# A rotary query projection at half its width: the half-exchanged columns made by ScalarE copies of the projected tile

## The reference

```
q = (_rms(c_q, q_norm) @ w_uq).reshape(bsz, L, MLA_HEADS, MLA_NOPE + MLA_ROPE)
q_nope, q_rope = q[..., :MLA_NOPE], q[..., MLA_NOPE:]
...
half = x.shape[-1] // 2
x1, x2 = x[..., :half], x[..., half:]
return jnp.concatenate([x1 * cos - x2 * sin, x1 * sin + x2 * cos], axis=-1)
```

## Time and profile before

| | |
|---|---|
| median of 3 runs | 3479.05 us |
| span of the profiled execution | 3477.8 us |
| TensorE matmul busy | 3399.0 us (98%), 16886 instructions |
| VectorE busy | 1670.0 us (48%) |
| ScalarE busy | 1424.7 us (41%) |
| GpSimd busy | 667.1 us (19%) |
| mean granted TensorE clock | 0.994 |

### The profile page before, as it was taken

One profiled execution on the slowest core, in us unless ns is written; L12 is line 12 of the kernel. 1 busy time (PEld: TensorE's weight loads), 2 busy tenths in 40 slices (PEclk: granted clock), 3 DMA queues, 4 the chain that ended last, 5 costly groups with the idle time before them and its releaser, 6 DMA issues. The chain is left out here.

```text
span 3477.8 us, 44891 instructions
## 1 busy us (share of the span) xinstructions
PE 3399.0 (98%) x16886; PEld 2804.8 (81%) x16886; DVE 1670.0 (48%) x3074; ACT 1424.7 (41%) x2495; POOL 667.1 (19%) x487
## 2 busy tenths in 40 slices
PE   7999999999899999999999999999999999999999
PEld 6788888877688888788787878788788888887887
DVE  4899999637555655521403232232323415555311
ACT  5233322243276666510325545445554234555200
POOL 4221212111201111033221111110102113331231
PEclk9999999999999999999999999999999999999999
DMA  4333323377421211543323232323322543333532
GB/s 129 91 88 91 100 83 97 100 210 233 134 53 38 57 43 39 155 135 104 129 68 104 88 111 78 117 66 90 105 82 88 186 154 118 109 109 116 182 97 66
DMA packets 431590, 368.88 MB, mean 106 GB/s; under 512 B 73560, under 2 KB 366936, under 8 KB 431376
## 3 DMA queue, kind: packets, MB, share of 16 engines
q1 hardware_dynamic: 345936, 271.62, 27.0%
q10 hardware_dynamic: 85440, 94.39, 7.8%
HBM read 238.18 MB, written 127.75 MB: 105 GB/s over the span
## 5 line engine op out<-in xcount | busy, mean ns | idle before, releaser
L874 PE MATMUL ef_ring<-ef_hhi,ef_whi 128*128 128x512 f32 x744 | 298.0, 400 | 2.0 <-issue 1.0
L2715 ACT ACTIVATE eow_w1raw<-of_ring 128x512 f32<-128x512 f32 x218 | 126.6, 595 | 415.2 <-PE of_ring L3088 414.2
L876 PE MATMUL ef_ring<-ef_hhi,ef_wlo 128*128 128x512 f32 x744 | 290.6, 391 | 0.0
L875 PE MATMUL ef_ring<-ef_hlo,ef_whi 128*128 128x512 f32 x744 | 290.4, 390 | 0.0
L400 POOL TENSOR_TENSOR ef_wlo<-ef_wraw,ef_whi 128x1024 fp32r<-128x1024 f32 x30 | 89.0, 2966 | 499.6 <-ACT ef_whi L449 499.6
L874 PEld LDWEIGHTS ef_ring<-ef_hhi,ef_whi 128*128 128x128 f32 x744 | 139.9, 188 | 42.6 <-issue 14.9
L2934 DVE SCALAR_TENSOR_TENSOR of_state<-of_state,of_small,of_tv 128x256 f32<-128x256 f32 x64 | 56.1, 877 | 245.6 <-ACT of_tv L2777 243.5
L511 ACT ACTIVATE ef_stage<-ef_ring 128x512 f32<-128x512 f32 x93 | 55.3, 594 | 273.2 <-PE ef_ring L876 273.0
L876 PEld LDWEIGHTS ef_ring<-ef_hhi,ef_wlo 128*128 128x128 f32 x744 | 139.9, 188 | 30.1
L875 PEld LDWEIGHTS ef_ring<-ef_hlo,ef_whi 128*128 128x128 f32 x744 | 140.3, 189 | 27.2
L3762 PE MATMUL mh_pf<-mh_v,mh_pp 128*128 128x258 f32 x736 | 162.0, 380 | 0.0
(11 more groups left out here) (612 smaller groups left out, 9460.2 us busy)
## 6 DMA issues: line engine op xcount, KB each, us to landing
of_wraw<-o_w_in SPq DMA_DIRECT2D x53, 512.0 KB, 3.9
ef_wraw<-e_w_in SPq DMA_DIRECT2D x29, 512.0 KB, 4.2
s_tmo<-eow_w1raw ACTq DMA_DIRECT2D x48, 256.0 KB, 2.3
ow_raw<-s_yt SPq DMA_DIRECT2D x18, 512.0 KB, 6.2
ow_raw<-o_w_out SPq DMA_DIRECT2D x16, 512.0 KB, 5.1
s_uc<-ef_stage ACTq DMA_DIRECT2D x24, 256.0 KB, 2.6
ef_ut<-s_uc SPq DMA_DIRECT2D x16, 384.0 KB, 4.1
s_za<-ef_stage ACTq DMA_DIRECT2D x24, 256.0 KB, 2.3
```

The lines of the kernel that those rows point to most:

```text
L874: pe.matmul(out, ah, hhi[:, f, tc], start=(f == 0), stop=False)
L875: pe.matmul(out, ah, hlo[:, f, tc], start=False, stop=False)
L876: mm = pe.matmul(out, al, hhi[:, f, tc], start=False, stop=(f == KT - 1))
L2715: act.activation(stage[i % 4][:, :], ring[i % 3][:, :] if i else start.first, func, scale=GK ** -0.5 if name == "q" else 1.0).then_inc(eva ...
```

## The change

The second group of each rotary item is gone. TensorE projects an item once, nine matmuls in place of eighteen. The weight columns are loaded in another order, so that the 128 partitions of the projected tile are first half of head 2p, first half of head 2p+1, second half of head 2p, second half of head 2p+1, 32 partitions each. The exchange is then a swap of the two blocks of 64 partitions. ScalarE does it with two copies of 64 partitions each, from the PSUM tile to r2, scaled by a column of signs (`rope_swap`), since the signs of the sine table stand in the old order. VectorE multiplies the PSUM tile by the cosines into r1 as before, then r2 in place by the sines, and adds. The sign column is set by three small VectorE instructions at the start of the stage, in a tile that is not yet in use. A load of the weights of a pair is four transfers of 32 columns in place of two of 128, and a load of a head's rotary query is four transfers of 32 partitions in place of two of 64.

```
--- before.py
+++ after.py
...
@@ -1345,8 +1343,8 @@
         y_out = [s.sem(f"y_out{u}") for u in range(3)]
 
         wn = d["w_uq_nope"].rearrange("(k p) n -> p k n", p=P)
-        wr = d["w_uq_rope"].rearrange("(k p) n -> p k n", p=P)
-        wsw = d["w_uq_swap"].rearrange("(k p) n -> p k n", p=P)
+        wr = d["w_uq_rope"].rearrange("(k p) (q a x i) -> q x a p k i", p=P, a=2, x=2, i=32)
+        sign = st[0][:, 0:1]
         wkv = d["e_w_ukv"].rearrange("(k p) n -> p k n", p=P)
 
         def cut(c):
...
@@ -1398,8 +1396,10 @@
                     if p >= 2:
                         sp.wait_ge(rhi_done, p - 1)
                         sp.wait_ge(rlo_done, p - 1)
-                    for x, src in enumerate((wr, wsw)):
-                        sp.dma_start(rraw[p % 2][:, x, :, :], src[:, :, p * P:(p + 1) * P]).then_inc(rw_in[p % 2], 16)
+                    for x in range(2):
+                        for a in range(2):
+                            at = 64 * x + 32 * a
+                            sp.dma_start(rraw[p % 2][:, :, at:at + 32], wr[p, x, a]).then_inc(rw_in[p % 2], 16)
 
                 def rope_store(p, c):
                     i = roped["r", p, c]
...
@@ -1410,8 +1410,10 @@
                     if h:
                         sp.wait_ge(qr_hi, 2 * h)
                         sp.wait_ge(qr_done, 2 * h)
-                    for a in range(2):
-                        sp.dma_start(qrr[64 * a:64 * a + 64, :], d["qr"][h * ROPE:(h + 1) * ROPE, :]).then_inc(qr_in, 16)
+                    for x in range(2):
+                        at = h // 2 * P + 64 * x + 32 * (h % 2)
+                        for a in range(2):
+                            sp.dma_start(qrr[64 * a + 32 * x:64 * a + 32 * x + 32, :], d["qr"][at:at + 32, :]).then_inc(qr_in, 16)
 
                 def place(m):
                     h, t, _ = tile_of(2 * m)
...
@@ -1486,8 +1488,8 @@
                     u = p % 2
                     pool.wait_ge(rhi_done, p + 1)
                     if p >= 2:
-                        pool.wait_ge(rope_mm, 6 * (p - 1))
-                    pool.tensor_tensor(rlo[u][:, :, :, :], rraw[u][:, :, :, :], rhi[u][:, :, :, :].bitcast(F32), ALU.subtract).then_inc(rlo_done, 1)
+                        pool.wait_ge(rope_mm, 3 * (p - 1))
+                    pool.tensor_tensor(rlo[u][:, :, :], rraw[u][:, :, :], rhi[u][:, :, :].bitcast(F32), ALU.subtract).then_inc(rlo_done, 1)
 
                 def key_split(i):
                     t = cut(chunk[i])
...
@@ -1551,10 +1553,20 @@
                     act.activation(whv[:, :, :, :], vraw[:, :, :, :], ACT.Copy).then_inc(vhi_done, 1)
 
                 def rope_high(p):
-                    act.wait_ge(rw_in[p % 2], 32 * (p // 2 + 1))
+                    act.wait_ge(rw_in[p % 2], 64 * (p // 2 + 1))
                     if p >= 2:
-                        act.wait_ge(rope_mm, 6 * (p - 1))
-                    act.activation(rhi[p % 2][:, :, :, :], rraw[p % 2][:, :, :, :], ACT.Copy).then_inc(rhi_done, 1)
+                        act.wait_ge(rope_mm, 3 * (p - 1))
+                    act.activation(rhi[p % 2][:, :, :], rraw[p % 2][:, :, :], ACT.Copy).then_inc(rhi_done, 1)
+
+                def rope_swap(x):
+
+                    i = roped[x]
+                    act.wait_ge(rope_mm, i + 1)
+                    if i >= 2:
+                        act.wait_ge(rope_done, i - 1)
+                    for a in range(2):
+                        of, to = slice(64 * (1 - a), 64 * (2 - a)), slice(64 * a, 64 * (a + 1))
+                        act.activation(r2[i % 2][to, :], ring[slot[x] % 3][of, :], ACT.Copy, scale=sign[of, :]).then_inc(swap_done, 1)
 
                 def project_high(x):
                     act.wait_ge(pj_mm, made[x])
...
@@ -1594,10 +1606,13 @@
                     act.activation(rope[:, x, :].rearrange("p (t n) -> p n t", t=CH), pos[:, x, :].rearrange("p (n t) -> p n t", t=CH), ACT.Copy
                                    ).then_inc(rope_set, 1)
                 value_high(0)
+                act.wait_ge(sign_set, 3)
+                rope_swap(opening[2])
                 rope_high(1)
                 latent_high(2)
-                for x in opening[2:]:
+                for x in opening[3:]:
                     if x[0] == "r":
+                        rope_swap(x)
                         if x[1] in (0, 1) and x[2] == 0:
                             rope_high(x[1] + 2)
                     else:
...
@@ -1655,11 +1670,11 @@
                     u = i % 2
                     if i >= 2:
                         dve.wait_ge(rope_out[u], 16 * (i // 2))
-                    for b, to in enumerate((r1[u], r2[u])):
-                        dve.wait_ge(rope_mm, 2 * i + b + 1)
-                        if i >= 2:
-                            dve.wait_ge(rope_done, i - 1)
-                        tt(by_position(to[:, :], c), by_position(ring[slot[x + (b,)] % 3][:, :], c), table(b, c), ALU.mult).then_inc(rope_mul, 1)
+                    dve.wait_ge(swap_done, 2 * i + 2)
+                    if i >= 2:
+                        dve.wait_ge(rope_done, i - 1)
+                    tt(by_position(r1[u][:, :], c), by_position(ring[slot[x] % 3][:, :], c), table(0, c), ALU.mult).then_inc(rope_mul, 1)
+                    tt(by_position(r2[u][:, :], c), by_position(r2[u][:, :], c), table(1, c), ALU.mult).then_inc(rope_mul, 1)
                     dve.wait_ge(rope_mul, 2 * i + 2)
                     tt(r1[u][:, :], r1[u][:, :], r2[u][:, :], ALU.add).then_inc(rope_done, 1)
 
...
@@ -1695,6 +1710,10 @@
                         dve.wait_ge(y_out[m % 3], 16 * (m // 3))
                     tt(y[m % 3][:, :], o[:, 0:256], zb[m % 3][:, :], ALU.mult).then_inc(y_done, 1)
 
+                dve.memset(sign, 1.0).then_inc(sign_set, 1)
+                dve.wait_ge(sign_set, 1)
+                for a in (0, 96):
+                    dve.memset(sign[a:a + 32, :], -1.0).then_inc(sign_set, 1)
                 first_low(0, slice(3, KC))
                 first_low(1, slice(0, 3))
                 latent_low(1)
...
@@ -1744,7 +1763,7 @@
                     if was[0] == "t":
                         pe.wait_ge(lo_done, before(was[1]) + was[2] + 1)
                     elif was[0] == "r":
-                        pe.wait_ge(rope_mul, 2 * roped[was[:3]] + was[3] + 1)
+                        pe.wait_ge(rope_mul, 2 * roped[was] + 1)
                     else:
                         pe.wait_ge(pl_done, made[was])
 
...
@@ -1777,10 +1796,9 @@
                     _, p, c = x
                     pe.wait_ge(rlo_done, p + 1)
                     pe.wait_ge(clo_done, chunk.index(c) + 2)
-                    for b in range(2):
-                        free(x + (b,))
-                        sums(ring[slot[x + (b,)] % 3][:, :],
-                             [((rhi[p % 2][:, b, k, :], rlo[p % 2][:, b, k, :]), (chi[:, k, cut(c)], clo[:, k, cut(c)])) for k in range(3)]).then_inc(rope_mm, 1)
+                    free(x)
+                    sums(ring[slot[x] % 3][:, :],
+                         [((rhi[p % 2][:, k, :], rlo[p % 2][:, k, :]), (chi[:, k, cut(c)], clo[:, k, cut(c)])) for k in range(3)]).then_inc(rope_mm, 1)
 
                 def scores(n, c):
                     h, t, (t0, ln) = tile_of(n)
```

More of the change, by code:

```diff
@@ L1284, in attention @@
     for x in opening:
[L1285 to L1288 removed]
+        ring_items.append(x)
+        if x[0] != "r":
             proj.append(x)
@@ L1319, in attention @@
             r1, r2 = ([o_.sb(f"{x}{u}", [P, 512]) for u in range(2)] for x in ("r1", "r2"))
-            rraw = [o_.sb(f"rraw{u}", [P, 2, 3, P]) for u in range(2)]
-            rhi, rlo = ([o_.sb(f"{x}{u}", [P, 2, 3, P], F32R) for u in range(2)] for x in ("rhi", "rlo"))
+            rraw = [o_.sb(f"rraw{u}", [P, 3, P]) for u in range(2)]
+            rhi, rlo = ([o_.sb(f"{x}{u}", [P, 3, P], F32R) for u in range(2)] for x in ("rhi", "rlo"))
         qrr = s.sb("qrr", [P, T])
```

24 lines of the change are left out of this document (10 added, 14 removed).

## The result

The changed kernel ran in 3469.12 us (median of 6 runs, 3467.34 to 3470.32), the kernel before beside it in 3480.53 (6 runs, 3478.23 to 3482.0): a ratio of 0.9966 with a 95% interval of 0.9955 to 0.9977, 11.4 us less. The forecast was 3465.5, with a range of 3461 to 3472; the value lies inside the range, but above the 3463 to 3468 that had been given 0.68. The first `peak`, forecast 14.6 earlier, came 11.56 earlier.

A forecast was written before the change was run, and what follows sets the result against it. TensorE was taken to bound the opening and main loop. Of 24.5 us removed, 14.6 would be gained at the first peak, less 1.0 at the seam: 3479.05 - 13.6 = 3465.5 us, range 3461 to 3472.

The forecast's parts named there:

- Step 1: Opening, before the value blocks: copy pairs of 1.07 us delay k02's low part; value blocks start at 901.3 instead of 903.88.
- Step 2: First value block to the addition of r00: takes 12.1 us instead of 11.2, so that addition starts at 913.4, 1.7 earlier.
- Step 3: Before r21: TensorE idles 5.3 us for GpSimd's split of the third weights; r21 starts at 922.45, 5.5 earlier.
- Step 4: Last six groups: 12.2 us plus 1.7 for the low clock; TensorE is through at 936.4 instead of 952.39.
- Step 5: Tail after r30: copies and VectorE's three instructions, partly slowed by GpSimd; first peak at 940.3, a gain of 14.6 us.
- all three bounds: Tail: limits by TensorE (939.4), VectorE (939.0 with half the contention) and stores (1.98 an item) lie within 0.3.
- Step 6: Seam to the main loop: TensorE waits 1.4 longer for the first exponential; 1.0 us taken off, leaving 13.6.
- rival B: Opening: fourth pair's weights land late and hold the swap of r21 4.9 us; gain 8.7, 3470.3; chance 0.12.
- Rival D: Main loop: a head's query loads, 32 partitions at a time, come too late; 3486 us; chance 0.05.
- Rival A: Opening: third weights do not hold TensorE, VectorE's nine items end at 936.6; gain 18.3, 3460.8; chance 0.08.
- C: Tail: GpSimd slows VectorE throughout, nine items take 29.3 us; gain 6.3, 3472.7; chance 0.07.
- the forecast's sign that later stages keep the distance: Stages after the opening: the forecast counts as wrong if they do not keep the lead won at the first peak.

The follow-up runs named there:

- e3: Changed kernel with ScalarE's copies (r2) written to two idle PSUM banks instead of SBUF; 3464.04 us.
- e4: Changed kernel with 22 filler matmuls into an unused bank during TensorE's wait for the third weights; 3469.1 us.
- e6: Changed kernel with GpSimd splitting the third weights right after the first key split, ahead of the second and third; 3469.46 us.
- e5: Changed kernel with the r2 in PSUM of e3 and 20 of the filler matmuls of e4; 3462.27 us.
- e10: Changed kernel with ScalarE's two copies made without the sign column as scale; 3467.51 us.
- e11: e7 (r2 in SBUF) with fourth weights loaded right behind the third, first query's loads behind the store of r10, GpSimd's order matching; 3467.93 us.
- e9: Changed kernel with a pair's weights loaded in one transfer of 512-byte pieces instead of four of 128-byte pieces; 3468.97 us.
- e7: e6 plus VectorE making the second and third rotary keys among the value blocks instead of ahead of r11; 3467.67 us.
- e8: e7 with the r2 in PSUM of e3 on the changed kernel; 3462.35 us.
- e12: e11 and e3 together on the changed kernel: r2 in PSUM, early keys and split, SyncE's order mended; 3459.9 us.

## Why the prediction came out as it did

The runs support this cause: where a VectorE instruction has both inputs in SBUF and GpSimd works beside it, both engines take longer, and the change gave VectorE's second product such inputs. That made two chains late, which end within 0.3 us of each other at the first `peak`. One is VectorE's own, from r11 on. The other is TensorE's: GpSimd's split of the third weights, the idle time before it, the low clock behind it.

e3 takes the contention away and wins 2.5. e4 and e6 relieve TensorE's chain alone, and nothing is won, since VectorE's is as long. e5 relieves both and wins 4.0. No run relieves VectorE's chain alone.

**Step 1** (copies, value blocks at 901.3): right in kind, 901.99 measured, after 3.07 idle where almost 4 were forecast. 0.70 of the delay was there before any copy: the table instructions behind q01 start at 889.94 for 889.24, since the stage began 0.3 later and k01 and q01 took 0.4 longer at the low clock. The pair took 1.39 in place of 1.07, 0.64 for the two pairs on the path; 0.35 of that is the sign operand (e10).

**Step 2** (addition of r00 at 913.4): 914.41. The late start of step 1 and one longer pair account for it.

**Step 3** (TensorE waits for GpSimd's split, r21 at 922.45): 924.12, after 6.44 idle for a forecast 5.3. The releaser was as named. VectorE's keys ended 0.9 later than forecast, and beside VectorE the key split took 1.59 for 1.29 and the split of the weights 1.45 for a forecast 1.15 (0.99 in e3). That this wait alone decides the end does not hold: e6 takes it away and wins nothing.

**Step 4** (TensorE through at 936.4): 939.19. The six groups took 15.07 for 13.9 forecast. By e4 this alone cost nothing, but the chain ended only 0.3 before VectorE's.

**Step 5** (the tail, VectorE from 919.3 to 940.3, 21.0 us) is the step that failed, and in its size: it took 23.1, from 920.24 to 943.35. The contention term had been taken as 2.4, half of a bound of 4.8 that rested on a doubling at most. Measured over these nine items: two second products 1.8 over 0.68 in sum (0.88, 2.25) and four additions 3.3 over 0.69 (1.41, 1.64, 1.38, 1.67), so 5.1. An instruction beside GpSimd is not doubled at most; it took up to 3.3 times as long here and 4.1 in e11. The Trainium skill (GPSIMD Engine Reference, Specifications) names instructions with two SBUF inputs among those that contend; that section gives no size. The trace agrees: every rotary product with a PSUM input stays within 693 ns, and every lengthened one has both inputs in SBUF. The other terms held: 17.3 of quiet work, and 0.7 in small gaps between the items where 0.9 had been taken. The sentence that all three bounds lie within 0.3 of each other held as well for VectorE's and TensorE's: the first came 4.3 us later than forecast, the second 3.6.

**Step 6** (1.0 lost at the seam): not lost. TensorE does wait longer at the loop's start, 3.46 for 1.82, but the lead grows from 11.56 to 11.77. So the 13.6 should have been the 11.6 of the first `peak` with nothing taken off; the two errors, 3.0 and 1.0, partly cancel, and that is luck. 0.7 of the 3.0 stood ahead of the first copy (step 1). The 3.6 us between forecast and median are 2.1 of gain and 1.5 by which the kernel before stood higher in six runs than in three.

**Edits at nothing:** the signs are hidden (written at 879.45, under the wait for the first latents), and rival B did not come: ScalarE waits for no late weight in the tail, and e9 finds no price for the small pieces. B's wait did appear in e7 and e8, where all but the loads had moved earlier. Rival D did not come either: the lead stays between 11.56 and 11.77 through the loop. Rival A did not come, since TensorE waited for the third weights; where e6 took that wait away, the nine items ended no earlier. C, GpSimd slowing VectorE throughout, held in part: 5.1 of its 12.1.

**Open.** Why later stages shift the distance of two executions by some 2 us at a time was not looked into, nor why the clock rises earlier in some runs of k01 and q01; so the forecast's sign that later stages keep the distance is not met by these two profiles, though it is by the medians. In e11 and e12 TensorE's first matmul came at 885.2 and 885.0 for 883.0, before any edited row; the stretch leaves that out, and why it came was not settled.

## What to carry to other kernels

TensorE work that is taken out counts only down to the next engine in line: 24.5 us went, 11.4 came back, and each holder relieved showed the next (GpSimd and VectorE in each other's way, then TensorE's low clock, then the written order of SyncE). Where two chains end together, an experiment that relieves one of them wins nothing and so can't say that the other is the only holder. When an edit moves an operand of VectorE from PSUM to SBUF, price it with GpSimd running beside it, not by the row in which GpSimd is still, and ask what waits for GpSimd, which is slowed too; a PSUM bank that is free in that stage is a scratch buffer without that price. Work that is moved earlier needs its stores and loads moved with it, so read the issue queue's order before promising the gain. A ruler for small edits should start as close to them as it can: here one that started 7 us earlier showed 0.3 and 0.8 us where 0.0 and 0.35 were won.

## What the runs showed of the hardware

- VectorE, 128x512 f32, two inputs in SBUF: 0.68 alone, up to 2.8 beside GpSimd (e11). With one input in PSUM: 0.67 to 0.69 beside the same work, in all the rotary rows of these runs. GpSimd is slowed as well: its subtraction of 128x384 took 1.45 beside such instructions and 0.99 with r2 in PSUM (e3).
- ScalarE, copy of 512 columns out of PSUM: 0.69 with a scale read from SBUF, 0.59 without; 0.69 for 64 partitions and for 128; two in a row add up in full (1.39, 1.21).
- Weight loads of 48 KB in 128-byte pieces landed in 2.0 to 5.9 us, in the median 2.6 (changed kernel); one load of 512-byte pieces in place of four won nothing (e9, short stretch 53.43 for 53.41).
- A granted clock of 0.86 cost nothing where another engine set the pace (e4), and about 1.5 us where TensorE was the holder (e3 to e5: short stretch 50.88 to 49.40).
